# Routing in a two-block transformer kernel: the sorted rows' weights computed by TensorE products instead of a scatter and a load, fewer counting products, and one token tile turned later

## The reference, cut to what matters

```python
def hier_moe(h, w_group, b_group, w_expert, b_expert, w_gate, w_up, w_down):
    ...
    group_logits = (t @ w_group).astype(jnp.float32) + b_group.astype(jnp.float32)
    group_probs = jax.nn.softmax(group_logits, axis=-1)
    _, gsel = lax.top_k(group_logits, 1)
    ...
    top_vals, top_idx = lax.top_k(in_group, TOP_K)
    weights = jax.nn.softmax(top_vals, axis=-1) * group_probs[rows, gsel][:, None]
    expert_ids = gsel[:, None] * EXPERTS_PER_GROUP + top_idx
    combine = jnp.sum(jax.nn.one_hot(expert_ids, N_EXPERTS, dtype=jnp.float32) * weights[..., None],
                      axis=1).astype(t.dtype)
    y = jnp.zeros_like(t)
    for e in range(N_EXPERTS):
        hidden = jax.nn.silu(t @ w_gate[e]) * (t @ w_up[e])
        y = y + combine[:, e:e + 1] * (hidden @ w_down[e])
    return y.reshape(bsz, s, d)
```

## Time and profile before

| what | value |
|---|---|
| median of 3 runs | 2445.9 us (2443.22 to 2448.65) |
| the profiled execution | 2447.59 us |
| its span, first to last instruction | 2445.5 us |
| PE busy | 2321.4 us (95%) |
| DVE, ACT, POOL busy | 1230.3, 758.3, 656.6 us |
| mean granted TensorE clock | 0.980 |
| chain that ended last | PE 81%, DVE 8%, DMA 5%, issue 3%, ACT 2%, POOL 1% |

### The profile page before, as it was taken

How to read it: one execution, slowest core, us unless ns; L and a number is a source line. 1 busy time by engine, 2 the same in 40 slices (tenths; PEclk the granted TensorE clock), 3 DMA queues, 4 the chain that set the end, 5 groups by cost and what they waited for, 6 DMA issues and landing times.

```text
span 2445.5 us, 30984 instructions
## 1 busy us (share of the span) xinstructions
PE 2321.4 (95%) x12572; PEld 1660.3 (68%) x12572; DVE 1230.3 (50%) x2156; ACT 758.3 (31%) x1194; POOL 656.6 (27%) x296
## 2 busy tenths in 40 slices
PE   8989787797999999999999999999999999999999
PEld 3334555564444477668878888888766887888887
DVE  4454555534556531874356677211287446677610
ACT  3344222222111143542233333223444223333311
POOL 0000000012000033124444444444313444444443
PEclk9999888898999999999999999999999999999999
DMA  5531000027999832113333333223211333333322
GB/s 217 136 76 35 19 2 2 2 83 270 364 409 409 346 133 86 52 53 98 99 91 97 97 95 95 86 95 107 86 53 56 99 95 95 95 95 95 98 81 97
DMA packets 80115, 287.54 MB, mean 118 GB/s; under 512 B 9283, under 2 KB 10307, under 8 KB 79334
## 3 DMA queue, kind: packets, MB, share of 16 engines
q1 hardware_dynamic: 76582, 279.29, 33.6%
q0 software_dynamic: 1408, 4.20, 0.4%
q10 hardware_dynamic: 1984, 2.06, 0.3%
HBM read 277.85 MB, written 16.07 MB: 120 GB/s over the span
## 4 chain that ended last, share of the span: by engine, by line
PE 81%; DVE 8%; DMA 5%; issue 3%; ACT 2%; POOL 1%; ACTq 0%; SPq 0%; DVEq 0%; another core or an unknown queue 0%; POOLq 0%
PE bank L1956 12%; PE bank L1958 12%; PE bank L1957 12%; PE bank L552 5%; DMA arena<-in_stream 4%; PE bank L2105 3%; PE bank L2106 3%; PE bank L2104 3%; DVE arena L417 3%; PE bank L1561 2%; PE bank L886 2%; PE bank L1941 2%; PE bank L1943 2%; PE bank L1942 2%; PE bank L1529 2%
## 5 line engine op out<-in xcount | busy, mean ns | idle before, releaser
L1691 POOL TENSOR_TENSOR ring_low<-ring,W_high 128x1024 fp32r<-128x1024 f32 x252 | 606.2, 2406 | 1118.2 <-ACT W_high L427 1118.2
L1956 PE MATMUL bank<-H_high,W_high 128*128 128x512 f32 x1408 | 556.1, 395 | 7.7 <-ACT arena L427 5.9
L1958 PE MATMUL bank<-H_high,ring_low 128*128 128x512 f32 x1408 | 549.1, 390 | 0.0
L1957 PE MATMUL bank<-H_low,W_high 128*128 128x512 f32 x1408 | 548.7, 390 | 0.0
L427 ACT ACTIVATE W_high<-ring 128x1024 fp32r<-128x1024 f32 x264 | 279.8, 1060 | 863.0 <-PE bank L1958 552.5
L1956 PEld LDWEIGHTS bank<-H_high,W_high 128*128 128x128 f32 x1408 | 264.6, 188 | 78.0 <-issue 23.0
L1957 PEld LDWEIGHTS bank<-H_low,W_high 128*128 128x128 f32 x1408 | 264.8, 188 | 55.9 <-issue 1.9
L1958 PEld LDWEIGHTS bank<-H_high,ring_low 128*128 128x128 f32 x1408 | 264.6, 188 | 56.0
L417 DVE TENSOR_TENSOR arena<-bank,root 128x512 f32<-128x512 f32 x116 | 79.7, 689 | 293.6 <-PE bank L1958 293.4
L427 ACT ACTIVATE arena<-bank 128x512 f32<-128x512 f32 (+4 forms) x183 | 79.4, 445 | 329.0 <-PE bank L851 120.4
L423 DVE SCALAR_TENSOR_TENSOR arena<-arena 128x512 f32<-128x512 f32 (+3 forms) x63 | 117.9, 1871 | 99.1 <-ACT arena L431 98.4
(11 more groups left out here) (276 smaller groups left out, 3242.6 us busy)
## 6 DMA issues: line engine op xcount, KB each, us to landing
ring<-in_stream SPq DMA_DIRECT2D x288, 512.0 KB, 3.6
arena<-in_stream SPq DMA_DIRECT2D x31, 2048.0 KB, 12.7
arena<-in_stream SPq DMA_DIRECT2D x31, 1024.0 KB, 10.3
sorted_x<-in_zero_row SPq DMA_DIRECT2D x4, 2048.0 KB
arena<-sorted_x SPq DMA_DIRECT2D x15, 512.0 KB, 16.2
X<-in_x SPq DMA_DIRECT2D x2, 1024.0 KB, 7.9
ring<-in_stream SPq DMA_DIRECT2D x1, 2048.0 KB, 19.5
out<-X SPq DMA_DIRECT2D x8, 256.0 KB, 6.9
```

What stands on the lines that cost most here:

```text
L1691: return G.tensor_tensor(ring_low[:, slot, :], ring[:, slot, :], W_high[:, s % 2, :].bitcast(F32), ALU.subtract)
L1956: mm(ps[:, :], wh[:, k, :], H_high[:, k, :], start=k == 0, stop=False)
L1957: mm(ps[:, :], wh[:, k, :], H_low[:, k, :], start=False, stop=False)
L1958: i = mm(ps[:, :], wl[:, k, :], H_high[:, k, :], start=False, stop=k == KD - 1)
```

## The change

Four edits, all in the routing.

1. The scatter to `sorted_w`, its clearing and its load are gone, with the three waits on them. Instead VectorE makes two small matrices per token tile and choice: `ROW_PLACED`, which marks the token's row within its pair, and `PAIR_WEIGHT`, its weight in the column of its pair; TensorE sums 8 products of them into `ROW_WEIGHT` (new job `rw`), between `px1` and `pxt0`.
2. The counts come from 5 products instead of 14: one with `BEFORE` over all four tiles at once, and for each tile one with ones, broadcast over all later blocks.
3. The last token tile is turned, and `ssq2` made, behind `pos` instead of ahead of it.
4. GpSimd no longer waits for `weights`, so its first scatter waits for `to_row`.

```diff
-    a += ["tsum", "lt"] + [f"ht{i}_{x}" for i in range(NT) for x in range(2)] + ["ssq2"]
-    a += ["pos", "px0", "px1", "pxt0", "pxt1"]
+    a += ["tsum", "lt"] + [f"ht{i}_{x}" for i in range(NT - 1) for x in range(2)]
+    a += ["pos"] + [f"ht{NT - 1}_{x}" for x in range(2)] + ["ssq2", "px0", "px1", "rw", "pxt0", "pxt1"]
...
-            for i_ in range(NT + 1):
-                for j in range(min(i_ + 1, NT)):
-                    i = mm(ps[:, i_ * NE:(i_ + 1) * NE], BEFORE if j == i_ else cc("ones"), mask[:, j, :],
-                           start=j == 0, stop=j == min(i_, NT - 1))
+            mm(ps[:, 0:NT * NE], BEFORE, RT("mask"), start=True, stop=False)
+            for j in (NT - 1, *range(NT - 1)):
+                later = ps[:, (j + 1) * NE:(NT + 1) * NE].rearrange("p (n e) -> p n e", e=NE)
+                i = mm(later, cc("ones"), mask[:, j:j + 1, :].to_broadcast([P, NT - j, NE]), start=False, stop=j == NT - 2)
             i.then_inc(pe.fills("pos"), 1)
+            turn_tokens(NT - 1)
+            pe.e.wait_ge(*pe.emptied("ssq2"))
+            mm(bank_of("ssq2")[:, :], cc("ones"), R2, start=True, stop=True).then_inc(pe.fills("ssq2"), 1)
...
+            pe.e.wait_ge(*pe.emptied("rw"))
+            pe.e.wait_ge(*pe.nth("pair_weights", 1))
+            for n in range(2 * NT):
+                i = mm(bank_of("rw")[:, 0:NPAIR], ROW_PLACED[:, n, :], PAIR_WEIGHT[:, n, :], start=n == 0, stop=n == 2 * NT - 1)
+            i.then_inc(pe.fills("rw"), 1)
...
             tt(RT("mask"), RT("oh1"), RT("oh2"), ALU.add).then_inc(dv.tells("mask"), 1)
+            for j in range(2):
+                both = RT(f"oh{j + 1}").rearrange("p (n e w) -> p n e w", n=NT, w=2)
+                V.tensor_reduce(ROW_OF_PAIR[:, NT * j:NT * j + NT], both[:, :, :, 1], AX.X, ALU.add).then_inc(dv.chained(), 1)
+                tt(PAIR_WEIGHT[:, NT * j:NT * j + NT, :], both[:, :, :, 0], both[:, :, :, 1], ALU.add).then_inc(dv.chained(), 1)
...
-            stt(RT("weight"), RT("weight"), 0.5, RT("over"), ALU.mult, ALU.mult).then_inc(dv.tells("weights"), 1)
+            st(stt(RT("weight"), RT("weight"), 0.5, RT("over"), ALU.mult, ALU.mult))
+            tt(PAIR_WEIGHT, PAIR_WEIGHT, RT("weight").unsqueeze(2).to_broadcast([P, 2 * NT, NPAIR]), ALU.mult).then_inc(dv.chained(), 1)
+            st(stt(ROW_OF_PAIR, ROW_OF_PAIR, float(ROWS // NE), RT("place"), ALU.mult, ALU.add))
+            tt(ROW_PLACED, cc("row_names").unsqueeze(1).to_broadcast([P, 2 * NT, P]), ROW_OF_PAIR.unsqueeze(2).to_broadcast([P, 2 * NT, P]),
+               ALU.is_equal).then_inc(dv.tells("pair_weights"), 1)
...
             rows_turned(dv, "pxt")
+            dv.e.wait_ge(*dv.filled("rw"))
+            V.tensor_copy(ROW_WEIGHT, bank_of("rw")[:, 0:NPAIR]).then_inc(dv.takes("rw"), 1)
...
-                    dv.e.wait_ge(ev("weights_in"), 16)
+                    dv.e.wait_ge(*dv.taken("rw"))
...
-            e.wait_ge(ev("rows_cleared"), 5 * 16)
-            po.e.wait_ge(*po.nth("weights", 1))
-            for n in range(2 * NT):
-                rows = RT("to_row")[:, n:n + 1].bitcast(I32)
-                nc.gpsimd.indirect_dma_start(sorted_w, bass.IndirectOffsetOnAxis(ap=rows, axis=0), RT("weight")[:, n:n + 1], None).then_inc(ev("weights_sorted"), 16)
+            e.wait_ge(ev("rows_cleared"), 4 * 16)
...
-            e.wait_ge(ev("weights_sorted"), 16 * 2 * NT)
-            e.dma_start(ROW_WEIGHT, sorted_w[0:ROWS, :].rearrange("(n p) w -> p (n w)", p=P), allow_slow_non_contiguous=True).then_inc(ev("weights_in"), 16)
```

More of the change, by code:

```diff
@@ L315, in build @@
         sorted_x = nc.dram_tensor("sorted_x", [ROWS + 2 * T, D], F32, kind="Internal").ap()
-        sorted_w = nc.dram_tensor("sorted_w", [ROWS + 2 * T, 1], F32, kind="Internal").ap()
         bias_scratch = nc.dram_tensor("bias_scratch", [DH, P * 640], F32, kind="Internal").ap()
@@ L683, in pe_A, with turn_tokens @@
             i.then_inc(pe.fills("lt"), 1)
-            for i_ in range(NT):
+            def turn_tokens(i_):
                 for x in range(2):
@@ L694, in pe_A @@
                     i.then_inc(pe.fills(job), 1)
-            pe.e.wait_ge(*pe.emptied("ssq2"))
-            mm(bank_of("ssq2")[:, :], cc("ones"), R2, start=True, stop=True).then_inc(pe.fills("ssq2"), 1)
+            for i_ in range(NT - 1):
+                turn_tokens(i_)
             pe.e.wait_ge(*pe.emptied("pos"))
@@ L1371, in build @@
         FIRST_PLACED = ch(12288, NT, P)
+        ROW_PLACED = early[:, 3072:3072 + 2 * NT * P].rearrange("p (n w) -> p n w", n=2 * NT)
+        PAIR_WEIGHT = RT("me").rearrange("p (n w) -> p n w", n=2 * NT)
+        ROW_OF_PAIR = RT("gpen")[:, 0:2 * NT]
         FIRST_ROWS = early[:, 5120:5120 + D]
@@ L2629, in sp_all @@
                     part = CLEARED_AT.index(s) * CLEARED_ROWS
-                    if part == 0:
-                        e.dma_start(sorted_w.rearrange("(n w) a -> n (w a)", w=D), ts_["zero_row"].to_broadcast([(ROWS + 2 * T) // D, D])).then_inc(ev("rows_cleared"), 16)
                     e.dma_start(sorted_x[part:part + CLEARED_ROWS, :], ts_["zero_row"].to_broadcast([CLEARED_ROWS, D])).then_inc(ev("rows_cleared"), 16)
```

## The result

The changed kernel takes 2429.6 us in the median (2428.5 to 2430.6, 4 runs) against 2445.8 us (2443.2 to 2448.7): ratio 0.9937, 95% interval 0.9923 to 0.9950, that is 16 us faster by these runs. Two further comparisons of the same kernel gave 0.9943 (0.9929 to 0.9957) and 0.9939 (0.9925 to 0.9952). The forecast was 12.5 us; 2433.5 was its time and 2429.5 to 2440 its range, so the time lies at the fast edge, 0.1 us inside it.

The account below looks back on a forecast made before the run. TensorE, busy 95% of the span, was taken as the bound, its idle gaps as the gain. First pair's start 1.75, wait for rows 8.23 and clock 2.5 sum to 12.5 us: 2433.5 us, range 2429.5 to 2440.

Parts of the forecast that it names:

- Counts: Routing's counting products, 5 for 14: VectorE reads the counts 1.5 us earlier (bounds 1.4 to 1.7).
- Last tile and `ssq2`: Moved behind the counts into TensorE's 4.82 us gap ahead of the placing products: zero cost.
- `px`: First pair's placing products on TensorE: 8.6 us instead of 10.03, a gain of 1.4 (bounds +2.9 and -4.1).
- `rw`: New weight products ahead of `pxt`: 1.9 us, net cost 1.15 (0.9 to 2.8) after filling a 0.73 us wait.
- First pair's start: First pair's products on TensorE start at 584.5 instead of 586.25, a gain of 1.75 us.
- Scatter: GpSimd's first issue of rows comes 14.4 us earlier; TensorE's 8.23 us wait for the second pair's rows goes.
- Clock behind the wait: TensorE's products after the wait for rows: 2.5 us won if no gap lowers the clock (bounds 0 and 2.7).
- What lies behind: From the end of the second pair's gate products to the span's end: moved earlier, same distance, 1826.6 us.
- (a): First pair gains nothing and the clock still drops: only 6.9 to 9.5 us won, 2436.4 to 2439; 18%.
- (b): VectorE holds up GpSimd's scatters: last lands 5.6 us later, TensorE waits 1.2 us, 2434.7 us; 8%.
- (c): Expert stage bound by its total bytes, so the stream takes the gain back: time stays at 2445.9 us; 4%.
- (d): Slower through the scatters' pitch: losing 4.9 us needs 4.0 us a scatter instead of 1.26; 2%.

Follow-up runs that it names:

- experiment 3: Kernel before with only the 5 counting products and the last tile and `ssq2` behind them; weights still scattered and loaded: 2444.3 us, ratio 0.9990.
- experiments 2: Changed kernel with 14 counting products and all tiles turned and `ssq2` made ahead of them, as before; weights still by products: 2433.7 us, ratio 0.9953.
- experiment 4: Changed kernel with the eight weight scatters and GpSimd's wait for weights put back ahead of the rows' scatters, load left out: 2440.5 us, ratio 0.9987.
- experiment 8: Changed kernel plus unused 512-column products on TensorE, two ahead of the counts, three ahead of `px`: 2431.1 us, ratio 0.9944.
- experiment 10: Changed kernel with the unused products of experiment 8 and `rw` split, four products ahead of `pxt` and four behind: 2427.6 us, ratio 0.9929.
- experiment 7: Kernel before plus five unused 512-column products in TensorE's 4.8 us gap ahead of `px`: 2441.0 us, ratio 0.9985.

## Why the prediction was right, point by point

Right in its direction, its cause and the size of its sum: 12.5 us were counted up to the end of the second pair's gates, 12.6 measured. The runs' gain was larger, 14.6 to 16.2 us by the medians, and 2429.6 us lies below the forecast's own range (2430.5 to 2436.5); it is inside the stated one by 0.1 us, which is luck.

- **Counts.** 1.5 us forecast, 1.05 measured. They began 8.75 us after the routing's start in both kernels, and VectorE was ready at 562.25, 10.2 us after it, 0.2 us sooner than forecast. But TensorE ran them mostly at 1.2 GHz (PEclk 0.94 over 560.5 to 561, 0.50 from there), and they took some 2.2 us (560.77 to 562.99) where I had estimated 1.75. So VectorE still waited 0.85 us: the term that was mis-sized is the half-clock price of the products.
- **Last tile and `ssq2`.** Zero, as forecast: they end at 565.45, with 2.36 us still idle behind them.
- **`px`.** 8.6 forecast, 8.77 measured. The forecast took the middle of two bounds, and that it fitted is luck. The clock, which the wide work in the gap was to keep up, fell with the counts, was back ahead of `ssq2`, and fell again 2.3 us after `ssq2`, just ahead of `px`:

```profile
561.00:561.50 0.50, 0.50 (x5) 0.50 (x4) 0.43 (x5) 0.00 (x0) 0.00 (x0) 0.50 1.03 410
...
564.50:565.00 0.50, 0.50 (x3) 0.12 (x2) 0.40 (x4) 0.44 (x2) 0.00 (x0) 1.00 1.02 410
...
567.50:568.00 0.50, 0.19 (x1) 0.22 (x2) 0.47 (x4) 0.00 (x0) 0.20 (x2) 0.76 0.10 41
```

- **`rw`.** 1.9 forecast, 1.70 from its start to that of `pxt`. Net of the wait that it fills, 1.15 forecast and 0.8 measured: from `px` to `pxt` are 10.31 us, and 9.54 in experiment 3, which has no `rw` and a `px` of 8.80. No wait in front; the weights were placed at 569.72, 6.7 us ahead.
- **First pair's start.** 1.75 forecast, 1.5 measured (28.27 us after the routing's start, 29.78 before).
- **Scatter.** 14.4 us earlier forecast, 13.9 measured. The rows' load went out 28.45 us after the start, where 29.1 were forecast (the flight was 4.6 us and not 6.5), and TensorE did not wait. The 8.23 us went whole (experiments 2 and 4).
- **Clock behind the wait.** 2.5 forecast, 2.7 measured.
- **What lies behind.** Here the prediction failed by 1.0 to 1.7 us. It took "all behind it" as moved and not changed. Both profiles of before have a fall of PEclk near 1030 us, the three of the changed kernel none. The kernel before, second profile, and the changed one, first profile, at the same place of the program:

```profile
1025.00:1030.00 5.00, 3.12 (x13) 1.84 (x11) 4.79 (x17) 2.72 (x7) 1.68 (x1) 0.87 0.36 105
1030.00:1035.00 5.00, 5.00 (x19) 3.23 (x19) 3.75 (x9) 0.49 (x1) 0.00 (x0) 0.79 0.02 5
```

```profile
1010.00:1015.00 5.00, 3.87 (x19) 2.40 (x17) 4.79 (x16) 3.44 (x7) 0.55 (x1) 1.00 0.30 86
1015.00:1020.00 5.00, 4.26 (x19) 2.96 (x21) 4.83 (x16) 1.39 (x5) 1.12 (x1) 1.00 0.07 24
```

With the 12.6 us this makes 13.6 to 14.3, and 14.0 to 14.6 is what matched executions differ by. The medians differ by 14.6 to 16.2, likely because each holds executions of both starts in its own mix. All fourteen profiles fit the fall: the seven that have one behind the stretch (before twice, experiments 2, 3, 4, 8 and 10, in 3 and 10 near 1800) need 1826.0 to 1826.7 us from there to the end, the seven without 1825.0 to 1825.9. But no experiment moved it by itself, and it does not go by the stretch: experiment 7 with 59.9 us had none, experiments 8 and 10 with 49.0 and 46.5 had one. So its cause is open.
- **Rivals.** (a) did not come: `px` was shorter and no gap lowered the clock behind `rows_over`. (b) cost 0.5 us of a spare that was larger: rows were asked for at 589.54 and their load issued at 580.47. The row that the prediction read for it was misread: the issue of 1.13 us at 574.43 was not beside the spreading copy, which had ended at 574.18. The first issue of a series took 1.13 or 1.14 us in thirteen of fourteen profiles, and 1.81 in experiment 4, where it met the end of the comparison and the whole copy. (c) is refuted: the distance to the end shrank. (d) is refuted: the mean pitch was 1.36 us, not 4.0.

## What to carry to other kernels

When an engine issues DMAs one by one, count issues and not bytes: eight that moved 4 KB took 10 us of GpSimd's queue ahead of the 4.2 MB that TensorE waited for. Values that are small and known on chip can be placed by a product with a one-hot matrix instead of a scatter and a load through DRAM; here they cost 0.8 us of TensorE's path, since a wait hid the rest, and splitting them over two waits won 0.8 us of the stretch back (not to be seen in the time). Compare two profiles by stretches between fixed points of the program and not by their spans: 4.45 us here were the execution's own.

## What the runs showed of the hardware

- An indirect DMA's issue on GpSimd took 0.95 us alone, at a pitch of 1.26, whether its rows were 4 bytes or 4 KB. The first of a series took 1.13. Wholly beside VectorE's copies inside SBUF one took 1.05 to 1.15, and 1.47 where it met the end of a comparison of 1024 columns and a whole copy. Two comparisons of 512 columns beside an issue left it at 0.95, which speaks for the copy as what lengthens it; no run had the comparison without the copy.
- PEclk fell to 0.50 some 0.5 us after TensorE's stop behind 14 products of 32 columns (before, stop at 568.50), but 2.4 us after its stop behind 24 transposes (changed kernel, 558.50) and 2.3 us after its stop behind `ssq2` (565.45). So the length of the gap alone did not tell when the clock fell, and no run separates what else did.
- In the one profile where TensorE was kept busy to hold the clock up in `px`, the gain was lost a step later: 1.7 us won in `px`, 1.7 lost in the products behind it (experiment 8). In experiment 10 both ran at 2.4 GHz.
